# Strassen operands of the two feed-forward inputs and of the first input summed from turned quarters

## What is computed

```python
h = rms_norm(x, norm_mix)            # "first input"
proj = h @ w_in                      # q, k, v of attention, q, k, v, gate of retention, two gates
...                                  # attention, retention, merge, out projection
h = rms_norm(x, norm_ffn)            # first feed-forward input (k = 2 in the kernel)
x = x + (silu(h @ w_gate) * (h @ w_up)) @ w_down
...                                  # second layer: attention, gating unit, out projection
h = rms_norm_2(x, g_pre_ffn)         # second feed-forward input (k = 4)
f = square(relu(h @ w_ff1)) @ w_ff2
```

## Time and profile before

| | us |
|---|---|
| median of 3 runs | 2598.3 (2596.51 to 2602.94) |
| profiled execution, its own time | 2598.22 |
| span of that execution in the trace | 2596.4 |
| granted TensorE clock, mean over the span | 0.997 of full |
| busy: PE, DVE, ACT, POOL | 2561.8, 1572.9, 1047.1, 1239.0 |

### The profile page before, as it was taken

How to read it: one execution, slowest core, us unless ns; L and a number is a source line. 1 busy time by engine, 2 the same in 40 slices (tenths; PEclk the granted TensorE clock), 3 DMA queues, 4 the chain that set the end, 5 groups by cost and what they waited for, 6 DMA issues and landing times.

```text
span 2596.4 us, 35463 instructions
## 1 busy us (share of the span) xinstructions
PE 2561.8 (99%) x13134; PEld 2139.7 (82%) x13134; DVE 1572.9 (61%) x2598; ACT 1047.1 (40%) x2073; POOL 1239.0 (48%) x988
## 2 busy tenths in 40 slices
PE   8999999999999999999999999999999999999998
PEld 6888888777888988888888878998888888888886
DVE  7355554685535554454698751168667666587787
ACT  4332343584223332332444541169733322254443
POOL 2478784354535565555221774448444544200204
PEclk9999999999999999999999999999999999999999
DMA  6557674705541222221752344323233333364534
GB/s 216 193 184 282 227 260 155 275 18 196 186 181 63 78 86 90 81 82 66 283 191 94 110 154 177 89 67 84 64 119 106 114 106 108 120 252 132 185 102 166
DMA packets 162711, 372.41 MB, mean 143 GB/s; under 512 B 21538, under 2 KB 42658, under 8 KB 158882
## 3 DMA queue, kind: packets, MB, share of 16 engines
q1 hardware_dynamic: 162540, 370.15, 41.7%
HBM read 268.01 MB, written 101.83 MB: 142 GB/s over the span
## 4 chain that ended last, share of the span: by engine, by line
PE 73%; DVE 3%; POOL 2%; DMA 1%; ACT 1%; issue 1%; POOLq 0%; SPq 0%; DVEq 0%; ACTq 0%
PE PS L841 9%; PE PS L844 9%; PE PS L843 9%; PE PS L906 6%; PE PS L907 6%; PE PS L908 6%; PE PS L650 3%; PE PS L652 3%; PE PS L651 3%; PE PS L672 3%; PE PS L675 3%; PE PS L674 3%; PE PS L1028 2%; PE PS L1017 1%; PE PS L977 1%
## 5 line engine op out<-in xcount | busy, mean ns | idle before, releaser
L2332 POOL TENSOR_TENSOR WL<-WRAW,WH 128x512 fp32r<-128x512 f32 (+1 forms) x149 | 248.4, 1668 | 310.8 <-ACT WH L1087 310.7
L841 PE MATMUL PS<-HH,WL 128*128 128x512 f32 (+1 forms) x976 | 369.0, 378 | 2.1 <-POOL WL L2332 2.1
L843 PE MATMUL PS<-HL,WH 128*128 128x512 f32 (+1 forms) x976 | 367.0, 376 | 0.0
L844 PE MATMUL PS<-HH,WH 128*128 128x512 f32 (+1 forms) x976 | 367.0, 376 | 0.0
L1604 DVE TENSOR_TENSOR WL<-TS,WH 128x512 fp32r<-128x512 f32 x228 | 235.6, 1042 | 193.5 <-ACT WH L1087 193.4
L906 PE MATMUL PS<-WH,DAL 128*128 128x512 f32 x756 | 294.7, 390 | 0.8 <-DVE WL L1878 0.8
L908 PE MATMUL PS<-WH,DAH 128*128 128x512 f32 x756 | 294.4, 389 | 0.0
L907 PE MATMUL PS<-WL,DAH 128*128 128x512 f32 x756 | 294.4, 389 | 0.0
L2516 POOL TENSOR_TENSOR X<-X,DV 128x512 f32<-128x512 f32 x56 | 90.1, 1634 | 354.4 <-DVE DV L1992 270.2
L1087 ACT ACTIVATE WH<-TS 128x512 fp32r<-128x512 f32 x228 | 138.4, 622 | 214.2 <-POOL TS L2348 214.1
L2348 POOL TENSOR_TENSOR TS<-WRAW 128x512 f32<-128x512 f32 x114 | 152.4, 1336 | 136.5 <-issue 132.9
(11 more groups left out here) (421 smaller groups left out, 6085.6 us busy)
## 6 DMA issues: line engine op xcount, KB each, us to landing
WRAW<-in_u_f SPq DMA_DIRECT2D x56, 512.0 KB, 3.6
WRAW<-in_u_in SPq DMA_DIRECT2D x54, 512.0 KB, 4.3
WRAW<-scr_t SPq DMA_DIRECT2D x52, 512.0 KB, 3.7
scr_h<-HS SPq DMA_DIRECT2D x96, 256.0 KB, 2.3
WRAW<-in_u_gu SPq DMA_DIRECT2D x44, 512.0 KB, 3.5
scr_t<-TTa SPq DMA_DIRECT2D x18, 1024.0 KB, 4.1
WRAW<-in_u_out SPq DMA_DIRECT2D x24, 512.0 KB, 3.6
scr_x<-X SPq DMA_DIRECT2D x24, 512.0 KB, 4.9
```

The lines of the kernel that those rows point to most:

```text
L841: e.matmul(PS[:, b, 0:wd], wl[:, blk(kk)], op_moving(q, kk, c0, wd, 0), start=(kk == 0), stop=False)
L843: e.matmul(PS[:, b, 0:wd], wh[:, blk(kk)], op_moving(q, kk, c0, wd, 1), start=False, stop=False)
L844: mm = e.matmul(PS[:, b, 0:wd], wh[:, blk(kk)], op_moving(q, kk, c0, wd, 0), start=False, stop=(kk == 3))
L2332: e.tensor_tensor(lo, raw, hi.bitcast(F32), ALU.subtract).then_inc(*c.inc("w_lo_p", i))
```

## The change

For k = 2 and 4 PE turns only the four quarters, 16 groups in place of 28. The banks of A21 are copied out whole by ACT (S3F); DVE forms S1, S3, S2 and S4 in turned form with the bank of A22, A11 or A12 as one source; ACT makes their high parts, POOL their low parts (`low_terms`). `row_sums`, `row_sum3`, `row_sum4` are gone. For k = 1 `turn0` is gone: POOL first forms A11 and A12 of j = 0 to 3 again as high plus low into X, eight operations ahead of its first `feed`; DVE's `sums0(j)` makes S3 and S2 with the banks of row block j + 4, which are freed only by that; POOL makes S4 and S1; ACT and DVE make high and low parts from X. ID is fetched ahead of row block 1.

```diff
-    TURN_AT = {i: 2 if i > 13 else 1 for i in range(6, 16)}
+    HIGH_AT = {4: [("S3", 0), ("S2", 0)], 5: [("S3", 1), ("S2", 1)], 6: [("S3", 2), ("S2", 2)], 7: [("S3", 3), ("S2", 3)],
+               9: [("S4", 0)], 10: [("S4", 1)], 11: [("S4", 2)], 12: [("S4", 3)],
+               13: [("S1", 0)], 14: [("S1", 1)], 15: [("S1", 2), ("S1", 3)]}
+    LOW_AT = HIGH_AT
...
-    TURN = ["A11", "S3", "S1", "S2", "S4", "A12", "A22"]
+    TURN = ["A21", "A22", "A11", "A12"]
+    LOWS = ["S3", "S1", "S2", "S4"]
...
-    AFTER_OUT = {8: 3, 9: 4, 10: 4, 11: 3}
-    AFTER_PROD = {0: [0, 0, 1, 1, 2, 2, 1], 1: [1] * 7}
+    AFTER_OUT = {7: 2, 8: 2, 9: 2, 10: 2}
+    AFTER_PROD = {0: [0, 1, 1, 1, 1, 0, 1], 1: [1, 1, 1, 0, 0, 0, 0]}
+    LOW_TERMS = [(q, j) for j in range(4) for q in LOWS]
+    LOW_OUT = {8: 1, 9: 3, 10: 1, 11: 3}
+    LOW_PROD = {0: [0, 0, 0, 1, 1, 1, 1], 1: [0, 1, 1, 1, 1, 0, 0]}
... PE
-            for _ in range(TURN_AT.get(i, 0)):
-                turn0(*turned0.pop(0))
-        for j in range(4):
-            turn0("S1", j)
... ACT, tile i of rv
+            if i == 4:
+                w.wait_ge(*c.at("n_x", (1, NT - 1)))
+            for q in HIGH_AT.get(i, ()):
+                high_term(*q)
... ACT, turn(k, q, j)
+            if q == "A21":
+                e.activation(op_whole(q, j), ps, ACT.Copy).then_inc(*bk.free(key))
+                return
+            e.activation(op_cols(q, j, 0), ps, ACT.Copy).then_inc(*c.inc("h_hi", key))
+            for sq in {"A22": (), "A11": ("S1",), "A12": ("S3", "S2", "S4")}[q]:
+                w.wait_ge(*c.at("s_ov", (k, j, sq)))
+                e.activation(op_cols(sq, j, 0), op_whole(sq, j), ACT.Copy).then_inc(*c.inc("h_hi", (k, sq, j)))
... DVE, back(1, tt)
+                lo.then_inc(*(c.inc("s_ov", (tt, b2)) if k == 1 and tt > 3 else bk.free(key)))
... DVE, sums0(j)
+            for half in range(2):
+                w.wait_ge(*c.at("s_op", (j, half)))
+            for b2 in range(2):
+                w.wait_ge(*c.at("s_ov", (j + 4, b2)))
+            for q, b2, left, right in (("S3", 0, whole0("A11", j), None), ("S2", 1, None, whole0("S3", j))):
+                key = "nb", 1, j + 4, b2
+                ps = by_tile(PS[:, bk.at(key), :])
+                e.tensor_tensor(whole0(q, j), ps if left is None else left, ps if right is None else right,
+                                ALU.subtract).then_inc(*bk.free(key))
+                w.wait_ge(*bk.out(key))
... DVE, turn(k, q, j)
+            if q == "A22":
+                w.wait_ge(*bk.out(("nb", k, "A21", j)))
+                operand("S1", ps, op_whole("A21", j), ALU.add)
+            elif q == "A11":
+                w.wait_ge(*c.at("s_ov", (k, j, "S1")))
+                operand("S3", ps, op_whole("A21", j), ALU.subtract)
+                operand("S2", op_whole("S1", j), ps, ALU.subtract)
+            else:
+                w.wait_ge(*c.at("s_ov", (k, j, "S2")))
+                w.wait_ge(*c.at(f"xs{j}", 1 if k == 2 else 3))
+                operand("S4", ps, op_whole("S2", j), ALU.subtract)
+            e.tensor_tensor(op_cols(q, j, 1), ps, op_cols(q, j, 0).bitcast(F32), ALU.subtract).then_inc(*bk.free(key))
... POOL, between its eight rsqrt and the rv tiles
+        for tt in range(4):
+            for half in range(2):
+                hh, hl = [t[:, 4 * half:4 * half + 4, blk(tt)].bitcast(F32) for t in (HH, HL)]
+                w.wait_ge(*bk.out(("nb", 1, tt, half)))
+                w.wait_ge(*bk.full(("nb", 1, tt, 1)))
+                e.tensor_tensor(whole0(("A11", "A12")[half], tt), hh, hl, ALU.add).then_inc(*c.inc("s_op", (tt, half)))
... POOL, tile i of rv
+            if 6 <= i < 10:
+                sums0(i - 6)
... POOL, feed-forward inputs
+        def low_terms(k, lows, n):
+            for _ in range(n):
+                q, j = lows.pop(0)
+                w.wait_ge(*c.at("h_hi", (k, q, j)))
+                if q in ("S1", "S2"):
+                    w.wait_ge(*c.at("s_ov", (k, j, "S2" if q == "S1" else "S4")))
+                e.tensor_tensor(op_cols(q, j, 1), op_whole(q, j), op_cols(q, j, 0).bitcast(F32),
+                                ALU.subtract).then_inc(*c.inc("s_op", (k, q, j)))
... SP
-            if t == 1:
                 e.dma_start(ID[:, :], a["c_id"]).then_inc(*c.inc("c_id", 0, 16))
```

More of the change, by code:

```diff
@@ L439, in bcast, with whole0, sum0_done @@
         return bass.AP(row.tensor, row.offset, [[0, P], [1, n]])
-    def rows0(q, j):
-        tt, half = {"S1": (j + 4, 1), "S2": (j, 0), "S3": (j + 4, 0), "S4": (j, 1)}[q]
-        return X[:, tt, hs(half)]
+    def whole0(q, j):
+        tt, half = {"A11": (j, 0), "A12": (j, 1), "S3": (j + 4, 1), "S2": (j + 4, 0), "S4": (j, 1), "S1": (j + 4, 0)}[q]
+        return by_tile(X[:, tt, hs(half)])
+    def sum0_done(q, j):
+        return bk.out(("nb", 1, j + 4, 0 if q == "S3" else 1)) if q in ("S2", "S3") else c.at("s_op", (1, j, q))
     def by_tile(rows):
@@ L598, in op_rows, with op_whole, op_done @@
     def op_rows(q, j):
-        return {"A11": HLF[:, 0:4, blk(j)], "A12": HLF[:, 4:8, blk(j)], "A22": HLF[:, 4:8, blk(j + 4)],
-                "S1": HLF[:, 0:4, blk(j + 4)], "S2": HHF[:, 4:8, blk(j + 4)], "S3": HHF[:, 0:4, blk(j + 4)],
-                "S4": HHF[:, 4:8, blk(j)]}[q]
+        return HLF[:, 4 * (q[2] == "2"):4 * (q[2] == "2") + 4, blk(j + 4 * (q[1] == "2"))]
+    def op_whole(q, j):
+        return {"S1": HLF[:, 0:4, blk(j + 4)], "A21": S3F[:, :, blk(j)], "S3": S3F[:, :, blk(j)],
+                "S2": S2F[:, :, blk(j)], "S4": by_tile(X[:, j, hs(1)])}[q]
+    def op_done(k, q, j):
+        if q[0] == "A":
+            return bk.out(("nb", k, q, j))
+        return c.at("s_ov", ("lo", q, j)) if k == 1 else c.at("s_op", (k, q, j))
     def op_cols(q, j, lo):
@@ L692, in normed @@
                 for b2 in range(2):
-                    w.wait_ge(*bk.out(("nb", k, tt, b2)))
+                    w.wait_ge(*(c.at("s_ov", (tt, b2)) if k == 1 and tt > 3 else bk.out(("nb", k, tt, b2))))
         back(1, 0)
@@ L1138, in act_program, with high_term @@
             first_square(4 + x)
[L1140 to L1145, removed]
+        def high_term(q, j):
+            if q == "S4":
+                w.wait_ge(*c.at("s_op", (1, j, "S1")))
+            if q == "S1":
+                w.wait_ge(*bk.full(("rv", 1, j + 4)))
+            w.wait_ge(*sum0_done(q, j))
+            e.activation(op_cols(q, j, 0), whole0(q, j), ACT.Copy).then_inc(*c.inc("h_hi", (1, q, j)))
         for i, key in enumerate(RVG):
@@ L1228, in act_program @@
                         w.wait_ge(*c.at(f"h11_{par(m)}", (0, m - 2)))
+                    else:
+                        for j in range(4):
+                            w.wait_ge(*c.at("s_ov", ("lo", "S1", j)))
                     w.wait_ge(*bk.full(key))
@@ L1674, in dve_program @@
                 sums0(i - 3)
-            for _ in range(TURN_AT.get(i, 0)):
-                turn0(*turned0.pop(0))
             if i < 15:
                 feed(key)
-        for j in range(4):
-            turn0("S1", j)
+            for q in LOW_AT.get(i, ()):
+                low_term(*q)
         nr, n1 = len(R1), len(A1)
@@ L2262, in dve_program @@
                 second_norm(OUTS[i - 1][1])
-                normed.append(OUTS[i - 1][1])
             if i in COMPLETE:
                 variance(4, tt, SS[0], VV[0])
-            if i - 1 in COMPLETE and len(normed) % 2 == 0:
-                row_sums(len(normed) // 2 - 1)
             turns(4, backs, AFTER_OUT.get(i, 0))
@@ L2481, in strassen @@
                     key = p, lay, m, c0
+                    if c0 == 0 and m in LOW_PROD:
+                        low_terms(k, lows, LOW_PROD[m][x])
                     if lay == 1 and m % 2 == 1 and p in DONE:
@@ L2674, in pool_program @@
                 rsqrt(4, tt, VV[0][:, tt:tt + 1], RR[0][:, tt:tt + 1])
-            if i - 1 in COMPLETE and rows % 2 == 0:
-                row_sum4(rows // 2 - 1)
             if i < 15:
                 feed(("o2", nh, tt))
+            low_terms(4, lows, LOW_OUT.get(i, 0))
             if i in SUMS_AT[2]:
                 sums_of_tiles(PAIR[2, SUMS_AT[2][i][0]], SUMS_AT[2][i][1])
-        row_sums(4, 3)
         def fin2(g, s):
```

115 lines of the change are left out of this document (34 added, 81 removed).

## The result

The changed kernel is slower. Its median is 2612.81 us (2610.17 to 2613.58), that of the kernel before on the same chip 2599.20 (2596.51 to 2602.94): a ratio of 1.0056 with a 95% interval of 1.0044 to 1.0068. The forecast was 2595.7, so the sign was wrong, and the range, which ended at 2606, missed it too. The profiled execution took 2610.17 us, span 2608.4, mean granted clock 0.994.

A forecast was written before the change was run, and what follows sets the result against it. PE, busy 99%, was taken to bound the kernel. Identity 0, rv tiles +12.5, first feed-forward input -5.5 and second -9.5 gave -2.5: 2595.7 us against 2598.2, range 2583 to 2606.

The forecast's parts named there:

- The chain of the rv tiles: Rv tiles: POOL's eight additions delay split, SP, ACT, DVE and banks; PE stops 14.7 and 2.5 us; stage +12.5.
- The clock after it: Behind the rv tiles' stops: lower clock bounded by 0 and 4.3 us, taken as 2.5.
- The price of a group of turns: On PE, each group of four turns costs 0.45 us; 16 groups removed from the first input save 7.2.
- the six groups less behind each out projection: Behind the out projection ahead of the second feed-forward input: six groups fewer give 2.7 us.
- Rival (a): Rv stage isn't held up and gives -7.2 us; total -22.2, 2576.0 us; chance 0.13.
- (b): Chain smaller, no clock loss, no stops left in second feed-forward layer: total -9.9, 2588.3 us; chance 0.15.
- two signs of being wrong: Prediction is wrong if PE's first stop is under 8 us or the clock is low anywhere over 10 us.
- Second feed-forward input: Its first half blocks gain 7.9 us, out projection 2.7, 1.1 set aside for the clock; stage sum -9.5.
- First feed-forward input: PE saves 5.4 us and a 0.43 wait; 0.3 taken for POOL's late S2; stage sum -5.5.
- POOL's eight further operations (S4, S1): Rv tiles: they cost nothing, POOL being idle about half the stage; without that cover 1.3 us each.
- The identity load: At the start, loading ID ahead of row block 1 costs between -0.3 and +0.4 us; taken as 0.
- (c): POOL's low parts bound the feed-forward first half blocks; layers +2.0 and -2.0; total +12.5, 2610.7 us; chance 0.12.

The follow-up runs named there:

- e1: Changed kernel with POOL making weight unit 6's low part ahead of the eight additions, not behind them; 2600.39 us, ratio 1.0015 to the kernel before.
- e2: e1 with DVE forming S3 and S2, which free two banks, ahead of the low parts of row blocks 6 and 7; 2593.82 us, ratio 0.9989.
- e11: e9 with the edits of e6 and e7, and the identity loaded behind row block 1 as in the kernel before; 2580.75 us, ratio 0.9936.
- e7: e2 with POOL's stage 0 down sums three products later, and ACT's turned high parts and weight split ahead of silu, relu and square; 2585.18 us, ratio 0.9954.
- e6: e2 with POOL's stage 0 down sums three products later, and the low part of S2 of j = 3 made by DVE, not POOL; 2592.70 us.
- e12: Kernel before with the edit of e7 alone, ACT's high parts and split ahead of silu, relu and square; 2596.98 us, ratio 0.9999.
- e3: Changed kernel with both feed-forward inputs as before; only the first input's part and the identity's place are changed; 2613.53 us, ratio 1.0066.
- e9: e2 with POOL's down sums behind the third product of stage 0 moved behind the eighth, their store two products later than in e2; 2589.83 us, ratio 0.9969.

## Why the prediction was wrong, step by step

**What was right.** The chain of the rv tiles, its cause and its size: 14.3 and 2.4 us for 14.7 and 2.5, and e1 and e2 showed both causes apart, POOL's order 10.7 us of the first stop, the ring of banks 3.6 and 2.4. The clock after it cost up to 3.5, not 2.5, since it was low after both stops. The price of a group of turns was right: e2 gained 6.6 us in spite of the identity's 0.7 and e11 7.4, for 7.2, and the six groups less behind each out projection gave 2.6 and 2.2 for 2.7 (the offset falls there from 16.7 to 14.1 and from 15.2 to 12.9). Rival (a) fell with the chain, (b) with the clock and the stops that it had at nothing. Neither of the prediction's two signs of being wrong, a first stop under 8 us and a low clock for over 10, came: it had looked for its error in the stage that it had right.

**Where it failed.** Four steps, in order of size.

1. *Second feed-forward input*, "two stops stay, 0.9 and 1.8 us, and perhaps 0.8 for POOL's S2", a gain of 7.9 less 1.1. The trace shows six stops, 2.25, 0.93, 1.00, 0.76, 0.46 and 1.64, 7.0 us where the sum had 3.5, and a low clock behind the first (0.63 of full from 1985.38 to 1990), which costs more than the 1.1 set aside. DVE was to finish the last norm 1.9 us earlier; it ended 11.3 us after P1 (1983.6, 1972.32), before 11.5. Its residual of that row took 2.29 us beside POOL's weight sums, which came about as late as before. From the norm to the bank of A12 of j = 2 DVE needed 10.0 us, nearly the 9.3 of the prediction's list of "some nine operations"; but the sum ends there, and behind it PE stops for DVE's product sums, 1.00 and 0.76, which stand behind a weight split that waits 0.79 us for ACT. e7 takes these two away and wins 2.3 us here; e6 wins 0.7. The largest stop, 2.25 us, no experiment touches. What ends just before it is a DVE split of 1.75 us beside a split of POOL's (1983.08 to 1984.73), where alone it takes 0.68; that the one holds up the other is likely, and the cause of this stop stays open. Nor was the base a typical one: its 35.2 us are 1.2 and 1.3 more than e12 and e3 take for the same blocks.
2. *First feed-forward input*, "it comes within 0.5 us of PE, either side. I take 0.3". Measured: five stops, 0.25, 0.99, 0.34, 0.46 and 1.64 us. "DVE has as many operations as before (7 for each j), ACT one more" was true and no argument: DVE frees the bank behind more operations, and ACT's order decides when it may begin. e7 gives 4.5 us here, e6 0.7.
3. *Nothing behind the rv tiles.* POOL's eight further operations (S4, S1) were said to "cost nothing", since "POOL is idle about half of this stage", and stage 0 was not looked at. POOL's loop there came another 3 us behind PE, and its reserve was 1.45. In e2, without the chain, POOL's last three rounds of down sums among the rv tiles still come 2.8, 3.7 and 4.2 us later than before (81.18, 96.12, 111.30 for 78.39, 92.45, 107.14), so it isn't the chain alone; no run takes the eight operations off POOL. This is also why rival (a) would have been wrong about its sum: with the stage free (e2), stage 0 took back 6.4 of 6.6 us. e9 gets 3.9 of them back by POOL's order.
4. *The identity load*, "between -0.3 and +0.4 us; I take 0": +0.7. One issue of 0.43 us had been counted; the block lands 0.66 later (ACT's square at 7.86 before, 8.52 after), and GB 0.3.

**The slower rival.** (c) gave 2610.7 us, near the 2612.8 measured, with +2.0 and -2.0 for the two layers. With their out projections they came to -0.5 and -4.2, and the rest of the total is from stage 0 and the start, which (c) didn't name. Its mechanism was wrong. It wanted low parts of 2.16 us each. In the first layer's half blocks they took 1.27 to 1.29, and 1.73 once. The Trainium skill, SBUF — State Buffer, "Who interferes with whom", has the rule that the prediction cites against this rival, more exactly: outside its two-port modes, a VectorE instruction with at most one SBUF input does not contend with GpSimd; one with two contends with a GpSimd instruction that reads SBUF. The trace agrees: the long ones there are DVE's weight splits, with both sources in SBUF (1.56 and 1.83 us in place of 0.68), while DVE's parts that read a bank stay at 0.68 beside POOL's low parts. So it is mostly DVE that paid, and e6 paid again, 1.17 us. The rival's time was near by luck: what came true in it is a stop for POOL's low part of S2, 1.64 us a layer, which e7, an edit of ACT's order, brings to 0.84 in the first layer and leaves as it is in the second.

**Sum.** 0.7 + 13.0 + 2.9 - 2.5 + 2.0 - 3.1 - 1.1 = +11.9, which is the span's 12.0. The forecast's terms for the same places gave -2.5.

## What to carry to other kernels

Where two engines hand work to each other through a third one's bank, count the waits in both directions for every round, not the operations: an operation that waits for the other side (here silu, for a product sum) belongs behind the one that the other side waits for. The wrong order cost nothing before the change (e12) and 7 us with it (e7). Before you call an engine's added work free because it is half idle, find its nearest dependent loop and that loop's reserve in us, here 1.45. And a gain on the bottleneck is kept only as far as the second-latest loop follows: look past the stage that you shorten.

## What the hardware showed that was not expected

- The same stop does not always lower the clock. After 2.44 us the changed kernel's granted clock was 0.50 from 68 to 70 us, and the first matmul's duration 0.76. In e1, after 2.44 us too, that matmul took 0.47 and the clock stayed at 1.00, though it had been low after the stop of 3.60 before:
```profile
46.00:50.00 4.00, 3.77 (x11) 0.60 0.00 0
56.60:60.00 3.40, 3.35 (x15) 1.00 0.75 263
```
  In e3 the stop of 2.44 us came once more, behind one of 14.54. PE began again at the full clock, 0.47 for the first matmul, and fell only then: matmuls last 0.63 and the granted clock is 0.50 from 69 to 72 us.
```profile
68.49 0.47 PE L678 MATMUL PS<-WH,HL 128*128 128x512 f32 x1 [2.44 <-DVE X L1660]
...
69.56 0.63 PE L678 MATMUL PS<-WH,HL 128*128 128x512 f32 x1
```
  So the clock fell behind two of three equal stops, at once or half a microsecond late. What decides it stays open; it is worth some 1.5 us here (seven starts of matmuls from 67.73 to 70.85, 3.1 us, where 7 x 0.23 is 1.6).
- In e6 an operation of DVE with two SBUF sources took 1.17 us beside POOL's of 1.3, in both layers. Moving work from a late POOL to DVE bought 0.7 us of the 1.64.
